# Rewriting the router of a hybrid encoder block: one selection sequence for groups and experts, rounded rank products, and a table built in two parts

## The reference, cut to what matters

```
g_sel = argmax(h @ rg_w + rg_b)                      # one of 4 groups
g_gate = softmax(g_logits)[g_sel]
top_v, top_i = top_k(e_logits[g_sel], 2)             # two experts of the group
gate = g_gate * softmax(top_v);  eid = g_sel * 8 + top_i
# the tokens of each expert are gathered, pass through the expert, and are summed with their gates
out[t] = sum over picks of gate * (silu(x @ w_gate[e]) * (x @ w_up[e])) @ w_down[e]
```

## Time and profile before

| what | us |
|---|---|
| three executions | 1740.64, 1743.70, 1748.39 (median 1743.7) |
| profiled execution, its own time | 1739.27 |
| its span, first to last instruction | 1737.5 |
| PE busy | 1561.2 (90%) |
| VectorE (DVE) busy | 622.4 (36%) |
| ScalarE (ACT) busy | 333.7 (19%) |
| POOL busy | 153.4 (9%) |

### The profile page before, as it was taken

The page is one execution under the profiler, slowest core; times in us unless marked ns, Lnnn a source line. Parts: engine busy times, 40 slices in busy tenths (PEclk is TensorE's granted clock), DMA queues, the critical chain, the costliest instruction groups (busy, mean ns, idle before and its releaser), DMA issues.

```text
span 1737.5 us, 18708 instructions
## 1 busy us (share of the span) xinstructions
PE 1561.2 (90%) x7051; PEld 862.8 (50%) x7051; DVE 622.4 (36%) x796; ACT 333.7 (19%) x596; POOL 153.4 (9%) x223
## 2 busy tenths in 40 slices
PE   6999999989999999579998898899889889889997
PEld 6587776768886445434333343333334334333433
DVE  3445656552224223623233133232313213332333
ACT  4222333342221233110101010010010111001010
POOL 1470055410000000000000000000000000000000
PEclk9999999999999999789999999999999999999999
DMA  7432322432216031359999999999999999999994
GB/s 268 121 90 80 92 59 68 156 118 98 97 49 266 1 121 49 145 238 421 422 421 422 421 422 422 421 422 422 422 422 422 422 422 421 422 421 420 419 422 187
DMA packets 114902, 484.37 MB, mean 279 GB/s; under 512 B 9410, under 2 KB 47404, under 8 KB 61868
## 3 DMA queue, kind: packets, MB, share of 16 engines
q1 hardware_dynamic: 110864, 470.84, 67.5%
q0 software_dynamic: 3264, 12.88, 2.0%
q10 hardware_dynamic: 732, 0.07, 0.0%
HBM read 484.81 MB, written 8.39 MB: 284 GB/s over the span
## 4 chain that ended last, share of the span: by engine, by line
PE 64%; DMA 21%; DVE 8%; ACT 3%; issue 2%; ACTq 0%; SPq 0%; DVEq 0%; POOL 0%; POOLq 0%
DMA weight_ring<-in_expert_w_up_dram 21%; PE ps L1878 17%; PE ps L1636 10%; PE ps L1514 8%; PE ps L1906 7%; PE ps L1745 3%; PE ps L1689 3%; PE ps L1855 3%; DVE residual L1396 3%; PE ps L1856 2%; PE ps L1465 2%; PE ps L1476 2%; ACT weight_ring L716 1%; DVE w_in_low L980 1%; PE ps L1456 1%
## 5 line engine op out<-in xcount | busy, mean ns | idle before, releaser
L1878 PE MATMUL ps<-weight_ring,transposed_acts 128*64 128x512 f32 x2048 | 469.0, 595 | 67.3 <-DMA weight_ring<-in_expert_w_up_dram 66.5
L1878 PEld LDWEIGHTS ps<-weight_ring,transposed_acts 128*64 128x64 f32 x2048 | 153.2, 137 | 377.1 <-issue 253.9
L1396 DVE TENSOR_TENSOR residual<-ps,residual 128x1024 f32<-128x1024 f32 x128 | 150.9, 1219 | 262.5 <-PE ps L1856 262.3
L1906 PE MATMUL ps<-weight_ring,transposed_acts 128*64 128x512 f32 x1024 | 226.8, 595 | 19.1 <-DVE transposed_acts L1403 19.1
L1414 DVE SCALAR_TENSOR_TENSOR y_low<-ps,proj_buffer,y_high 64x1024 fp32r<-64x1024 f32 x64 | 82.1, 1283 | 211.3 <-ACT y_high L881 210.3
L1906 PEld LDWEIGHTS ps<-weight_ring,transposed_acts 128*64 128x64 f32 x1024 | 71.8, 137 | 155.4 <-issue 152.5
L881 ACT ACTIVATE y_high<-ps,proj_buffer 64x1024 fp32r<-64x1024 f32 x64 | 70.9, 1108 | 306.2 <-PE ps L1906 305.4
L1855 PE MATMUL ps<-y_high,spread 128*128 128x512 f32 x256 | 113.9, 445 | 14.5 <-DVE residual L1396 10.5
L1514 PE MATMUL ps<-mix_high,w_in_high 128*128 128x512 f32 x288 | 116.6, 405 | 1.3 <-issue 1.3
L873 ACT ACTIVATE transposed_acts<-ps 128x512 f32<-128x512 f32 x32 | 19.1, 598 | 494.4 <-PE ps L1878 494.4
L1514 PE MATMUL ps<-normed_low,w_in_high 128*128 128x512 f32 x288 | 112.3, 390 | 0.0
(11 more groups left out here) (260 smaller groups left out, 1690.9 us busy)
## 6 DMA issues: line engine op xcount, KB each, us to landing
weight_ring<-in_expert_w_gate_dram SPq DMA_DIRECT2D x128, 1024.0 KB, 24.0
weight_ring<-in_expert_w_up_dram SPq DMA_DIRECT2D x128, 1024.0 KB, 25.9
weight_ring<-in_expert_w_down_dram SPq DMA_DIRECT2D x128, 1024.0 KB, 19.0
weight_ring<-in_w_in_dram SPq DMA_DIRECT2D x18, 1024.0 KB, 5.6
weight_ring<-in_w_out_dram SPq DMA_DIRECT2D x16, 1024.0 KB, 5.0
weight_ring<-in_xkv_w_dram SPq DMA_DIRECT2D x8, 1024.0 KB, 6.0
residual<-in_x_dram SPq DMA_DIRECT2D x8, 1024.0 KB, 16.0
weight_ring<-in_xq_w_dram SPq DMA_DIRECT2D x4, 1024.0 KB, 9.5
```

Source lines behind the costliest of these rows:

```text
L1396: v.tensor_tensor(part, ps[:, bank:bank + 2, :].rearrange("p b n -> p (b n)"), part, ALU.add).then_inc(sum_ready if last else part_added, 1)
L1878: ins = mm(ps[side * SLOTS:(side + 1) * SLOTS, 0, :], xsT[:, k, par * SLOTS:(par + 1) * SLOTS], w[:, kk, :], start=(k == 0), stop=(k == KD ...
L1906: ins = mm(ps[half, 4 + n // 2, :], act_t[:, f * SLOTS:(f + 1) * SLOTS], w[:, n * 512:(n + 1) * 512], start=(f == 0), stop=(f == KF - 1), ...
```

## The change

Groups and experts are chosen in one sequence. The logits are laid out as 5 sets of 8 for each token (4 groups of experts and the group logits padded with a large negative number), and `first_of` works on all 20 sets of a partition at once; the chosen group then masks the result. The rank products become five fp32r products, the first over all token tiles and the total at once. The place of a pick is one number, 64 times the block plus the slot, and is split into the two by adding and subtracting a large constant that rounds it. Both picks go through each operation together, and a scan takes the place of five shifted additions. The table is built in two runs of products: tokens first (fp32r), gates after them (fp32). The first gather takes its row numbers straight from the token part. The new fp32r tiles lie over the memory keys and values, which are dead by then. POOL clears half as much before the gather, and earlier; three small copies go to ScalarE; the ramp `tramp` is written behind the first gather. In the diff, lines that are only renames, declarations or order of columns are left out, and so is the body of the old rank arithmetic, which stands above.

```diff
+        with ExitStack() as shared:
+            tri_r = shared.enter_context(nc.sbuf_tensor("lower_triangle", [P, P], F32R))
+            ones_r = shared.enter_context(nc.sbuf_tensor("ones_rounded", [P, P], F32R))
+            M_r = shared.enter_context(nc.sbuf_tensor("picks_of_token", [P, NT + 1, NE], F32R))
+            P_r = shared.enter_context(nc.sbuf_tensor("slot_of_pick", [P, 2 * NT, SLOTS], F32R))
+            shared.enter_context(nc.sbuf_tensor("below_block_tokens", [P, 96], F32))
+            Bv_r = shared.enter_context(nc.sbuf_tensor("block_tokens", [P, 2 * NT, TCOL], F32R))
...
+        L = vx[:, :, :].rearrange("p m n -> p (m n)")[:, 512:512 + NT * (NG + 1) * EPG].rearrange("p (t c) -> p t c", t=NT)
...
+            link(g.iota(io[:, :], pattern=[[1, 64]], base=0, channel_multiplier=0,
+                        allow_small_or_imprecise_dtypes=True))
+            link(g.iota(tok[:, :], pattern=[[P, NT]], base=0, channel_multiplier=1,
+                        allow_small_or_imprecise_dtypes=True))
+            link(g.tensor_scalar(io64[:, :], io[:, :], float(SLOTS), None, ALU.mult))
+            link(g.tensor_scalar(tok[:, :], tok[:, :], -float(ABSENT), None, ALU.add))
...
-            for b in range(2):
-                pool.wait_ge(hn_stored[b], 32)
-            pool.wait_ge(h_turned, 4 * 14)
-            g.memset(hs[:, :, :], 0.0).then_inc(xs_clear, 1)
+            pool.wait_ge(hn_stored[0], 32)
+            pool.wait_ge(h_turned, 4 * 13)
+            g.memset(hs[:, 0, :], 0.0).then_inc(xs_clear, 1)
+            pool.wait_ge(xo_part, NT)
+            g.memset(L[:, :, :], NEG).then_inc(logits_padded, 1)
             pool.wait_ge(xs_clear, 1)
-            pool.wait_ge(table_ready, 1)
+            pool.wait_ge(hn_stored[1], 32)
             xs = hs[:, 0, :]
-            g.iota(tramp, pattern=[[1, S]], base=0, channel_multiplier=0,
-                   allow_small_or_imprecise_dtypes=True).then_inc(tramp_ready, 1)
             def gather(pair):
-                column, copied, turned_ = pair * 2, pair + 1, pair * 4
+                column, copied, turned_ = pair * 2, pair, pair * 4
                 if not isinstance(pair, int):
                     copied, turned_ = pool.to_reg(copied), pool.to_reg(turned_)
-                wait_past(pool, xs_turned, turned_)
-                g.tensor_copy(cols[:, 0:1], tokf[:, ds(column, 1)]).then_inc(idx_copied, 1)
-                pool.wait_ge(table_ready, 1)
-                pool.wait_ge(idx_copied, copied)
+                if isinstance(pair, int) and pair == 0:
+                    pool.wait_ge(first_ids, 2)
+                else:
+                    wait_past(pool, xs_turned, turned_)
+                    g.tensor_copy(cols[:, 0:1], tokf[:, ds(column, 1)]).then_inc(idx_copied, 1)
+                    pool.wait_ge(table_ready, 1)
+                    pool.wait_ge(idx_copied, copied)
                 g.indirect_dma_start(out=xs, out_offset=None, in_=hn_dram,
                                      in_offset=bass.IndirectOffsetOnAxis(ap=cols[:, 0:1], axis=0),
                                      bounds_check=S - 1, oob_is_err=False).then_inc(gathered, 16)
             gather(0)
+            pool.wait_ge(table_ready, 1)
+            g.iota(tramp, pattern=[[1, S]], base=0, channel_multiplier=0,
+                   allow_small_or_imprecise_dtypes=True).then_inc(tramp_ready, 1)
             gather(1)
...
+            act.wait_ge(tri_ready, 1)
+            act.wait_ge(xs_done, NT)
+            a.activation(tri_r[:, :], tri, ACT.Copy).then_inc(rounded_ready, 1)
+            a.activation(ones_r[:, :], ones[:, :], ACT.Copy).then_inc(rounded_ready, 1)
+            a.activation(M_r[:, NT, :], io[:, 0:NE], ACT.Copy, scale=0.0).then_inc(rounded_ready, 1)
...
+            a.activation(sm[:, 4, 0:1], eps[:, 0:1], ACT.Exp)
...
+            dve.wait_ge(logits_padded, 1)
+            v.tensor_tensor(L[:, :, 0:NCOL], ps[:, 4, 0:NT * NCOL].rearrange("p (t c) -> p t c", c=NCOL),
+                            wide(rbias[:, :].unsqueeze(1), P, NT, NCOL), ALU.add).then_inc(logits_ready, 1)
+            dve.wait_ge(logits_ready, 1)
+            sets = NT * (NG + 1)
+            ramp_e = wide(io[:, 0:EPG].unsqueeze(1), P, sets, EPG)
+            def first_of(vals, best, pick):
+                best, ti = best.rearrange("p t s -> p (t s)"), r["ti"].rearrange("p t s -> p (t s)")
                 link(v.tensor_reduce(best, vals, AX, ALU.max))
+                link(v.tensor_tensor(pick, vals, wide(best.unsqueeze(2), P, sets, EPG), ALU.is_equal))
+                link(v.scalar_tensor_tensor(out=r["cand"], in0=pick, scalar=-64.0, in1=ramp_e, op0=ALU.mult, op1=ALU.add))
+                link(v.tensor_reduce(ti, r["cand"], AX, ALU.min))
+                link(v.tensor_tensor(pick, r["cand"], wide(ti.unsqueeze(2), P, sets, EPG), ALU.is_equal))
+            values_ = L[:, :, :].rearrange("p t (s e) -> p (t s) e", e=EPG)
+            first_of(values_, r["m1"], r["h1"])
+            link(v.scalar_tensor_tensor(out=r["t8"], in0=r["h1"], scalar=NEG, in1=values_, op0=ALU.mult, op1=ALU.add))
+            first_of(r["t8"], r["m2"], r["h2"])
...
+            def of_groups(name):
+                return r[name].rearrange("p (t s) e -> p t s e", s=NG + 1)[:, :, 0:NG, :]
+            gh = r["h1"].rearrange("p (t s) e -> p t s e", s=NG + 1)[:, :, NG, 0:NG]
+            gh_e = wide(gh.unsqueeze(3), P, NT, NG, EPG)
+            link(v.tensor_tensor(r["both"], r["h1"], r["h2"], ALU.add))
+            v.tensor_tensor(M_r[:, 0:NT, :].rearrange("p t (g e) -> p t g e", e=EPG), of_groups("both"), gh_e,
+                            ALU.mult).then_inc(picks, 1)
+            link(v.tensor_tensor(r["dtg"], r["m2"][:, :, 0:NG], r["m1"][:, :, 0:NG], ALU.subtract))
+            link(v.tensor_tensor(r["dtg"], r["dtg"], gh, ALU.mult))
+            v.tensor_reduce(r["dt"], r["dtg"], AX, ALU.add).then_inc(top_done, 1)
+            v.tensor_tensor(r["gs"], L[:, :, NE:NCOL], wide(r["m1"][:, :, NG].unsqueeze(2), P, NT, NG),
+                            ALU.subtract).then_inc(gmax_done, 1)
+            for k in range(2):
+                link(v.tensor_tensor(r["M"][:, k].rearrange("p t (g e) -> p t g e", e=EPG), of_groups("h1" if k == 0 else "h2"),
+                                     gh_e, ALU.mult))
+            dve.wait_ge(ranks, 1)
+            R = ps[:, 5, 0:NT * NE].rearrange("p (t e) -> p t e", e=NE)
+            link(v.tensor_scalar(r["near"], ps[:, 5, NT * NE:(NT + 1) * NE], SLOTS / 2 - 0.5, ROUND, ALU.add, ALU.add))
+            link(v.tensor_scalar(r["over"], r["near"], -(ROUND + SLOTS), 0.0, ALU.add, ALU.max))
+            link(v.tensor_tensor_scan(r["upto"], ones[:, 0:NE], r["over"], 0.0, ALU.mult, ALU.add))
+            link(v.scalar_tensor_tensor(out=r["base"], in0=r["upto"], scalar=float(SLOTS * (NE - 1)), in1=r["over"],
+                                        op0=ALU.add, op1=ALU.subtract))
+            link(v.tensor_tensor(r["diff"], io64[:, 0:NE], r["base"], ALU.subtract))
+            link(v.tensor_tensor(r["beyond"], R, wide(r["base"].unsqueeze(1), P, NT, NE), ALU.add))
+            link(v.scalar_tensor_tensor(out=r["inside"], in0=R, scalar=float(SLOTS),
+                                        in1=wide(r["diff"].unsqueeze(1), P, NT, NE), op0=ALU.is_lt, op1=ALU.mult))
+            link(v.tensor_tensor(r["place"], r["beyond"], r["inside"], ALU.add))
+            link(v.tensor_tensor(r["sel"], r["M"], wide(r["place"].unsqueeze(1), P, 2, NT, NE), ALU.mult))
+            link(v.tensor_reduce(r["at"], r["sel"], AX, ALU.add))
+            link(v.tensor_scalar(r["bkn"], r["at"], -(SLOTS / 2 - 0.5), ROUND, ALU.add, ALU.add))
+            link(v.tensor_scalar(r["bk"], r["bkn"], -ROUND, None, ALU.add))
+            link(v.tensor_tensor(r["row"], r["at"], r["bk"], ALU.subtract))
+            v.tensor_tensor(P_r[:, :, :], wide(io[:, 0:SLOTS].unsqueeze(1), P, 2 * NT, SLOTS),
+                            wide(r["row"].rearrange("p k t -> p (k t)").unsqueeze(2), P, 2 * NT, SLOTS),
+                            ALU.is_equal).then_inc(slot_onehot, 1)
+            link(v.tensor_tensor(r["one"], wide(io64[:, 0:TCOL].unsqueeze(1), P, 2 * NT, TCOL),
+                                 wide(r["bk"].rearrange("p k t -> p (k t)").unsqueeze(2), P, 2 * NT, TCOL), ALU.is_equal))
+            v.tensor_tensor(Bv_r[:, :, :].rearrange("p (k t) c -> p k t c", k=2), r["one"].rearrange("p (k t) c -> p k t c", k=2),
+                            wide(tok[:, :].unsqueeze(1).unsqueeze(3), P, 2, NT, TCOL), ALU.mult).then_inc(block_onehot, 1)
             dve.wait_ge(gexp_done, 1)
...
             link(v.tensor_reduce(r["gsum"], r["eg"], AX, ALU.add))
             link(v.reciprocal(r["gg"], r["gsum"]))
             dve.wait_ge(texp_done, 1)
-            link(v.tensor_scalar(r["w2"], r["et"], 1.0, None, ALU.add))
-            link(v.reciprocal(r["w2"], r["w2"]))
-            link(v.tensor_tensor(r["w1"], r["gg"], r["w2"], ALU.mult))
```

(43 more changed lines are left out.)

136 lines of the change are left out of this document (28 added, 108 removed).

## The result

| | executions | median us | ratio to before (95%) |
|---|---|---|---|
| before | 4 | 1745.17 (1740.64 to 1748.39) | |
| changed | 4 | 1727.05 (1722.51 to 1729.10) | 0.9894 (0.9863 to 0.9925) |

The kernel is 18.1 us faster by the medians, and the interval of the ratio (13 to 24 us) lies clear of no change. One further execution of the kernel before, in e9_before, took 2702.46 us at a mean granted clock of 0.556 and stands outside every comparison. The first profiled execution of the changed kernel took 1729.10, with a span of 1727.3; that is only 10.2 us less than the span before. The timeline of the changed kernel through the router says why. Its rows answer to the earlier trace rows: first logits operation, picks, first use of the ranks, token one-hots, ids, gather, transposes.

The account below looks back on a forecast made before the run. The start of the expert weight stream, behind a serial 41.3 us router stretch, was taken to fix the end. Gains .8 + 4.6 + 8.3 + 1.7 + 2.6 = 18.0 us off the 1743.7 median gave 1725.7, range 1718 to 1733.

Parts of the forecast that it names:

- A: Choice of group and experts on VectorE: from 5.67 to 4.91 us, gain .76.
- E: Unpacking to the start of the gather: from 3.79 to 1.2 us, gain 2.6, up to 3.5.
- F: Gather and transposes, up to the first expert product: 8.70 us, as before.
- the gain isn't passed on: Rival: the weight stream's start does not fix the end; time 1740 to 1744 us, chance .06.
- a slower pace of pairs: Rival in the expert loop: 15 pairs each longer, 1.8 us per pair needed to be slower; chance .03.
- C: Places and one-hots on VectorE: from 13.66 to 5.33 us, gain 8.3.
- B: Rank products, VectorE's end to its use of them: from 6.41 to 1.84 us, gain 4.6 (4.0 to 5.1).
- D: Table products up to the first copy from PSUM: from 3.09 to 1.35 us, gain 1.7 (.2 to 2.5).
- F2: From the first matmul of the gathered rows' transposes to the first expert product; 4.20 us before, not forecast separately.
- The covers: Gates, ramp, fills and ScalarE copies cost nothing, hidden beside other work; gates leave TensorE free .7 to 2.1 us in time.
- Rival 2: New waits bite: short rounded products at their ceilings, or gates late by 1.6 us; 1727 to 1731 us, chance .13.
- Rival 3: More than summed: gate products raise TensorE's clock, or gather starts at once (.9); gain some 20.5 us, chance .08.

Follow-up runs that it names:

- e9_before: The kernel before, run again with no edit: median 1743.47 us over nine compared executions, ratio 0.9991 to before.
- e5_fp32: Changed kernel with rank and token products in fp32 instead of fp32r: ranks part 2.68 us in place of 1.48, token products part 2.18 in place of 1.28.
- e1_again: The changed kernel run again with no edit: five executions, median 1726.97 us, ratio 0.9903 to before.
- e10_stretch_fill: Changed kernel plus unread TensorE products in the router's serial stretch only (3, 5, 2 and 3 of them): median 1722.86 us, ratio 0.9870 to before.
- e11_sixteen: Changed kernel plus 16 unread 32 by 32 transposes on TensorE ahead of the ranks: one execution, serial stretch 23.18 us.
- e4_late_gather: Changed kernel with the first gather again behind the whole table and the token ramp: median 1731.31 us, ratio 0.9925 to before.
- e3_delayed: Changed kernel plus 80 linked VectorE operations behind the ranks, 18 us of delay: median 1748.14 us, ratio 1.0015 to before.

## Why the prediction was right, point by point

The gain forecast was 18.0 us, the medians give 18.1. The stretch gives 17.3 and 17.6 in the two profiles of the changed kernel. Its parts A to E gave 18.2 where 18.0 was forecast, and F took back 0.9 and 0.6, where nothing was forecast. That the medians meet the forecast to 0.1 us is luck: single executions of one kernel lie 7 to 12 us apart. That the gain is 17 to 18 us, and where it comes from, is not.

- **What bounds.** Right: 18.07 us put back into the stretch cost 21.2, and the loop lasts 858.3 and 858.8 us between its second and last pair in the two kernels. That the gain isn't passed on, and a slower pace of pairs, are both out.
- **A**, forecast 4.91, is 4.92; **C**, forecast 5.33, is 5.43. The price of .19 + n/960 held for every linked operation of the two parts but the scan, of two PSUM readers too. The scan took .23 for its 32 columns, where I had .19. The rest of C's miss is a slip in the sum: the token product of 400 columns stands there with .50 to its end, where the price gives .57, and it took .57; the slot one-hot delays the next by .61 as priced. C is nearly half the gain (8.2).
- **B**, forecast 1.84 with bounds 1.3 and 2.45, is 1.48. The term was mis-sized because I took the ranks at 1.6 and they were on VectorE's side after 1.33: a rounded short product costs .24 to .27 at clock 0.50, not near the .44 of an fp32 one. e5_fp32 shows the .44 for fp32, the mean of four products with 128 to 32 columns.
- **D**, forecast 1.35, is 1.28. **E**, forecast 1.20, is 1.30 (.33 for the two operations, and .97); the .94 ahead of the gather did not go with the index copy, since as much stands behind a wait on VectorE. So the upper bound of 3.5 for E's gain was not reached. (All high ends as they stand add up to 20.2, not 20.5; nothing hangs on it.)
- **F**, forecast unchanged at 8.70, is 9.64 and 9.32. This is the step that failed, by .6 to .9 us. I had looked for an engine that holds up the gather. The rows' packets came at most 0.4 us later; TensorE began late, with a fetch of instructions in the wait, and its transposes ran at 0.50 as before. F2 is .15 to .26 longer, which no run explains.
- **The covers.** All held. The gate products ended at 737.45, 2.6 before the transposes; the ramp was written at 738.6; the fills were done at 712.7, 7.6 before the logits operation, and in e1_again, where the logits came early, at 711.0, 2.7 before, near the 2.8 forecast; the transposes of the next tile on VectorE took .69 beside the fill. ScalarE's three copies ended at 681.9, 2.4 before its next operation that waits for VectorE, with the load of 1.28 that always stood there in between. Rival 2 (new waits bite) did not come.
- **The rule on the shared ports.** The fill no longer met a TENSOR_SCALAR, so its 3.31 us did not return. The Trainium skill ("SBUF — State Buffer", section "Who interferes with whom") says that copies can take the ports which GpSimd needs to write a gather's descriptors. No run here shows that: 16 copies of 512 fp32 columns, at .46 each, beside the gather's issue (1.09 with and without them) did not delay it, nor the rows. So to charge nothing was right.
- **Rival 3** had the right place. The low clock through the stretch was worth some 1.7 us (e10_stretch_fill against e11_sixteen), but it took fillers to get them; the gate products alone did not raise it, and the gather did not start at once (.97).

## What to carry to other kernels

When an ordered chain of small operations stands ahead of a stream that cannot be prefetched, count its linked operations and price them by two or three rows: here that was good to 0.1 us for the two parts on VectorE, of 5 and 14 us before. Where nothing else is prefetched, the gain of the whole is the gain of the chain. Before two profiles are compared, cut both at the same events: here spans differed by 10 us where the change was worth 17, because one profile had drawn a fall of TensorE's clock ahead of the part in question. And give an otherwise idle TensorE something to do through such a chain, if its next work is on the path.

## What the runs showed of the hardware that I had not expected

- The granted clock fell to 0.50 twice ahead of or in the router in every profile, of either kernel, but not at the same moment: in the 14 profiles the first fall began between 659 and 663 us, the second between 707 and 717, and the last logits came anywhere from 712.88 to 721.98. The profiled executions of the changed kernel differ by just that much; that the scatter of the unprofiled ones has the same cause is likely, not shown.
- A fetch of instructions (one packet on q8) in TensorE's wait for the gathered rows went with a start 0.4 to 0.9 us late (4.86 to 5.29 against 4.30 to 4.52); 16 further instructions ahead of it moved it away.
- The first indirect gather begins 0.94 to 1.0 us after the end of the operation that releases it, on POOL (0.94, before) or on VectorE (0.97 to 1.0), and an IOTA of 0.56 fits into that time at no cost (e4_late_gather). Later gathers begin 0.83 to 0.85 after POOL's own copy.
- Short rounded products at clock 0.50: five with 160 to 32 columns and weights of 128 by 128 took 1.2 us, eight with 50 columns and weights of 128 by 64 took 1.02; in fp32 2.4 and 1.92.
- TensorE's clock can come back after its next work has begun: the first expert products took 14.0 us behind most stretches, and 16.24 in e3_delayed, where the clock was 0.50 until 767, over 4 us into them.
